# Head roots by logarithm, hyena chunks in quarters, and a convolution and spectrum products straight from PSUM, in the second block of a two-block model

## The reference

```
q = apply_rope_2(split_heads_norm(q, q_norm, 8 heads), cos, sin)     # RMS norm over 128 per head
k = apply_rope_2(split_heads_norm(k, k_norm, 2 heads), cos, sin)
p = softmax(q @ concat(k_ctx, k).T * 128**-0.5);  attn = p @ concat(v_ctx, v)

def short_conv(u, w, bias):                     # three taps, per channel, over tokens
    up = pad(u, one token on each side)
    return up[:, :-2] * w[0] + up[:, 1:-1] * w[1] + up[:, 2:] * w[2] + bias
def hyena_mix(u, ...):
    x0, x1, v = split(short_conv(u, conv_w, conv_b), 3)   # 3 x 512 channels
    v = v * x1
    y = irfft(rfft(v, 512) * rfft(filter, 512))[:256] + v * bias    # complex product
    return y * x0
merged = sigmoid(g_a) * (attn @ w_o_attn) + sigmoid(g_h) * (hyena @ w_o_hyena)
```

## Time and profile before

| what | value |
|---|---|
| median of 3 runs | 2690.96 us (2687.08 to 2691.71) |
| profiled execution, its own time | 2687.02 us |
| its span | 2685.1 us |
| PE busy | 2540.7 us (95%) |
| DVE, ACT, POOL busy | 1263.0, 1266.3, 1472.4 us |
| chain that ended last | PE 81%, DVE 9%, ACT 4%, POOL 3% |

### The profile page before, as it was taken

The page is one execution under the profiler, slowest core; times in us unless marked ns, Lnnn a source line. Parts: engine busy times, 40 slices in busy tenths (PEclk is TensorE's granted clock), DMA queues, the critical chain, the costliest instruction groups (busy, mean ns, idle before and its releaser), DMA issues.

```text
span 2685.1 us, 42027 instructions
## 1 busy us (share of the span) xinstructions
PE 2540.7 (95%) x16564; PEld 2180.6 (81%) x16564; DVE 1263.0 (47%) x2162; ACT 1266.3 (47%) x2111; POOL 1472.4 (55%) x857
## 2 busy tenths in 40 slices
PE   6999999998999899999898999989999988989997
PEld 6997889988998789986576766766888867888997
DVE  7795744452975755444466422132101037635223
ACT  5467854355447963453533311342333344535543
POOL 6875746458975855454431123743555544463970
PEclk9999999999999999998999999999999999999999
DMA  5443343354544343353320112231222223135554
GB/s 222 179 173 142 114 155 140 142 188 170 183 167 157 110 173 142 112 191 126 141 79 32 48 64 78 94 114 66 94 94 94 95 108 110 70 120 189 174 188 142
DMA packets 50552, 347.63 MB, mean 129 GB/s; under 512 B 5312, under 2 KB 8640, under 8 KB 8896
## 3 DMA queue, kind: packets, MB, share of 16 engines
q1 hardware_dynamic: 47840, 340.31, 35.2%
q10 hardware_dynamic: 2528, 4.72, 0.5%
HBM read 343.96 MB, written 1.05 MB: 128 GB/s over the span
## 4 chain that ended last, share of the span: by engine, by line
PE 81%; DVE 9%; ACT 4%; POOL 3%; issue 2%; DMA 1%; SPq 0%; POOLq 0%; ACTq 0%; DVEq 0%
PE pg L1838 21%; PE pg L1839 20%; PE pg L1840 20%; PE pg L1863 2%; PE ps L2127 2%; POOL ring_lo L643 2%; PE ps L2148 2%; PE ps L2146 1%; PE pg L1861 1%; PE ps L2286 1%; ACT ring_hi L755 1%; PE ps L1959 1%; PE ps L2358 1%; DVE big L1669 1%; PE ps L2267 1%
## 5 line engine op out<-in xcount | busy, mean ns | idle before, releaser
L643 POOL TENSOR_TENSOR ring_lo<-ring,ring_hi 128x1024 fp32r<-128x1024 f32 (+3 forms) x500 | 1167.3, 2348 | 803.7 <-ACT ring_hi L755 803.5
L1838 PE MATMUL pg<-HH,ring_hi 128*128 128x256 f32 (+1 forms) x3360 | 1077.9, 321 | 54.4 <-DVE HL L1309 16.3
L1839 PE MATMUL pg<-HH,ring_lo 128*128 128x256 f32 (+1 forms) x3360 | 1031.8, 307 | 0.0
L1840 PE MATMUL pg<-HL,ring_hi 128*128 128x256 f32 (+1 forms) x3104 | 958.7, 309 | 0.0
L1838 PEld LDWEIGHTS pg<-HH,ring_hi 128*128 128x128 f32 x3360 | 643.1, 191 | 138.5 <-issue 68.5
L1839 PEld LDWEIGHTS pg<-HH,ring_lo 128*128 128x128 f32 x3360 | 644.4, 192 | 42.9 <-issue 14.8
L1840 PEld LDWEIGHTS pg<-HL,ring_hi 128*128 128x128 f32 x3104 | 595.2, 192 | 30.8
L755 ACT ACTIVATE ring_hi<-ring 128x1024 fp32r<-128x1024 f32 (+6 forms) x564 | 555.0, 1002 | 33.6 <-DMA ring<-in_w_stream_dram 32.8
L765 ACT ACTIVATE take<-pg 128x256 f32<-128x256 f32 (+1 forms) x268 | 113.7, 425 | 497.7 <-PE pg L1840 446.3
L1840 PE MATMUL pg<-big_r,ring_hi 128*128 128x256 f32 (+1 forms) x864 | 275.3, 319 | 0.0
L1838 PE MATMUL pg<-big_r,ring_hi 128*128 128x256 f32 (+1 forms) x736 | 241.1, 328 | 7.3 <-DVE big_r L1778 3.1
(11 more groups left out here) (324 smaller groups left out, 3371.6 us busy)
## 6 DMA issues: line engine op xcount, KB each, us to landing
ring<-in_w_stream_dram SPq DMA_DIRECT2D x320, 1024.0 KB, 4.8
hn<-in_consts_dram ACTq DMA_DIRECT2D x2, 1024.0 KB, 5.9
cst<-in_consts_dram SPq DMA_DIRECT2D x1, 1472.0 KB, 19.6
prm<-in_params_dram SPq DMA_DIRECT2D x1, 1110.0 KB, 7.4
X<-in_xT_dram SPq DMA_DIRECT2D x1, 1024.0 KB, 5.8
X<-in_ctxT_dram ACTq DMA_DIRECT2D x1, 1024.0 KB, 5.7
out_dram<-H ACTq DMA_DIRECT2D x1, 1024.0 KB, 4.8
cst<-in_consts_dram SPq DMA_DIRECT2D x1, 768.0 KB, 16.5
```

What stands on the lines that cost most here:

```text
L643: pool.tensor_tensor(ring_lo[:, slot, cols], ring[:, slot, cols], ring_hi[:, place * P:(place + n) * P].bitcast(F32), SUB).then_inc(sem(LO ...
L1838: first = pe.matmul(out, a[0], b[0], start=start, stop=False)
L1839: pe.matmul(out, a[1], b[0], start=False, stop=False)
L1840: return first, pe.matmul(out, a[0], b[1], start=False, stop=stop)
```

## The change

**Head roots.** The square root and the reciprocal of the three head norms of a block-two layer become a logarithm and an exponential with scale -0.5, both on ACT (the way block one already had). `log_exp_tables` asks for the table set ahead of each root.

**Order.** The rope of K moves behind q2 chunk 4, those of heads 0 to 3 behind v2 chunk 0, the last two behind hy2 chunks 1 and 2. PE waits for earlier ropes before it writes the sums of the next norm, since both use `ps`. The third norm's sum moves from v2 chunk 1 to v2 chunk 2.

**Quarters.** The hy2 chunks beside attention are given out in quarters of two tiles; five of the 32 quarters go to the first two steps, the rest is spread.

**Convolution.** ACT writes the middle tap with its bias straight to the destination (Identity with scale and bias); DVE adds the two outer taps with `pg` as an operand. `hraw` and its padding go. A bank of `pg` is now free when DVE's convolution is done (`hconv`), not when ACT has drained it.

**Spectrum.** `VFT` is `ps` itself; ACT's copy goes.

```diff
 def att2_fill(l):
-    return spread([("hy2", l, j) for j in range(EARLY_HY, 12)], STEPS2[l] + LAG + 1)
+    parts = []
+    for j in range(EARLY_HY, 12):
+        x = ("hy2", l, j)
+        parts += [("part", x)] * (n_parts("hy2") - 1) + [x]
+    points = STEPS2[l] + LAG + 1
+    return [parts[0:3], parts[3:5]] + spread(parts[5:], points - 2)
...
-        VFT = hn[:, :].rearrange("p (a b) -> p a b", a=4)
+        VFT = ps[:, :, :]
...
-        ROPES_AFTER = [[0], [1], [2], [3, 4]]
+        ROPES_AFTER = [[], [3], [4], []]
...
             def hyena_in(l, j):
                 n, ns = N_TOK[l], N_SEQ[l]
-                ahead(CHUNK["hy2", l, j])
-                if 12 * l + j >= 2:
-                    act.wait_ge(sem("hconv"), 12 * l + j - 1)
-                s0 = (j % 2) * 2
-                act.activation(hraw[:, s0:s0 + ns, 1:T + 1],
-                               ready(CHUNK["hy2", l, j])[:, 0:n].rearrange("p (s t) -> p s t", s=ns), ACT.Copy)\
-                    .then_inc(sem("drained"), 1)
+                w = (l * 12 + j) * HY_TAPS
+                act.activation((X0, X1, VX)[j // 4][:, j % 4, 0:n], ready(CHUNK["hy2", l, j])[:, 0:n], ACT.Identity,
+                               bias=PR("conv_b", l * 12 + j), scale=PR("conv_w", w + 1)).then_inc(sem("hy_first"), 1)
...
-                elif by_log(i):
+                else:
                     inverse_root(hn[:, 0:cols], ps_flat[:, 0:cols], eps6, scale, "hn_rms")
-                else:
-                    act.activation(hn[:, 0:cols], ps_flat[:, 0:cols], ACT.Sqrt, bias=eps6, scale=scale).then_inc(sem("hn_rms"), 1)
...
-                    act.wait_ge(sem("vf_ready"), 2 * l + s + 1)
-                    act.activation(VFT, ps[:, :, :], ACT.Copy).then_inc(sem("vf_done"), 1)
...
-                    if not by_log(i):
-                        link(dve.reciprocal(r, r))
...
-                link(dve.tensor_scalar(dst, hraw[:, s0:s0 + ns, 0:T], PR("conv_w", w), PR("conv_b", l * 12 + j), MUL, ADD))
+                link(dve.scalar_tensor_tensor(dst[:, :, 1:T], src[:, :, 0:T - 1], PR("conv_w", w), dst[:, :, 1:T], MUL, ADD))
                 yield
-                link(dve.scalar_tensor_tensor(dst, hraw[:, s0:s0 + ns, 1:T + 1], PR("conv_w", w + 1), dst, MUL, ADD))
-                yield
-                ins = dve.scalar_tensor_tensor(dst, hraw[:, s0:s0 + ns, 2:T + 2], PR("conv_w", w + 2), dst, MUL, ADD)
+                ins = dve.scalar_tensor_tensor(dst[:, :, 0:T - 1], src[:, :, 1:T], PR("conv_w", w + 2), dst[:, :, 0:T - 1], MUL, ADD)
...
-                    dve.wait_ge(sem("vf_done"), k + 1)
+                    dve.wait_ge(sem("vf_ready"), k + 1)
...
+                    elif name == "hy2":
+                        pe.wait_ge(sem("hconv"), 12 * l + i + 1)
...
+                def rot2(jj):
+                    pe.wait_ge(sem("hn_done"), i + (1 if jj == 0 else 2 if jj < 3 else 3))
+                    rot(ROPE2[l] + jj, C("rot2"), Q2_[:, 2 * jj - 2:2 * jj, 0:T] if jj else K2_[:, :, 0:T])
                 for j in range(8):
                     chunk("q2", l, j, KD, hx, n)
                     if j == 1:
                         head_norm(i, 1024)
+                    if j == 4:
+                        rot2(0)
                     if j == 5:
                         pe.wait_ge(sem("hn_rms"), i + 1)
+                        pe.wait_ge(sem("rope"), ROPE2[l] + 1)
                         head_norm(i + 1, 4 * n)
...
-                    if tt == 1:
+                    if tt == 0:
                         pe.wait_ge(sem("hn_rms"), i + 2)
+                        rot2(1)
+                        rot2(2)
+                    if tt == 2:
+                        pe.wait_ge(sem("rope"), ROPE2[l] + 3)
                         head_norm(i + 2, 4 * n)
```

More of the change, by code:

```diff
@@ L282, in chunk_order @@
         add("hy2", 0, EARLY_HY)
-        out += sum(att2_fill(l), []) + sum(hyena_fill(l), [])
+        out += whole(sum(att2_fill(l), [])) + sum(hyena_fill(l), [])
         add("oh", 0, 16)
@@ L302 @@
 for x in ORDER:
-    count += x[0] != "dn"
+    count += x[0] not in ("dn", "hy2")
     DRAINED[x] = count
@@ L573, in build @@
         MGQ = H[:, :, T:2 * T]
-        ROPES_AFTER = [[0], [1], [2], [3, 4]]
+        ROPES_AFTER = [[], [3], [4], []]
         FILTER_1 = [0, 2, 4, 6, 7]
         FILTER_2 = [0, 1, 2, 3, 4]
-        def by_log(i):
-            return i < HN_BASE2[0]
         def in_place(i):
-            return by_log(i) and i % 6 != ATT_N
+            return i < HN_BASE2[0] and i % 6 != ATT_N
         def x_done(i, m=KD - 1):
@@ L715, in _ @@
                 for h in range(HEADS if l == DEPTH - 1 else 0):
-                    done = sum(att2_fill(l)[:(HIGH_AT + [ATT_STEPS + LAG])[h] + 1], [])
+                    done = whole(sum(att2_fill(l)[:(HIGH_AT + [ATT_STEPS + LAG])[h] + 1], []))
                     if done:
@@ L1159, in _ @@
                         attention2_exp(IT2_BASE[l] + k, steps[k][1])
-                    drain_fill(items)
+                    drain_fill(whole(items))
                     if LAG <= k < len(steps) + LAG:
@@ L1707, in hyena_conv @@
                 n, ns = N_TOK[l], N_SEQ[l]
[L1708 to L1710 removed]
+                dve.wait_ge(sem("hy_first"), 12 * l + j + 1)
+                dst, src = (b.rearrange("p (s t) -> p s t", s=ns) for b in ((X0, X1, VX)[j // 4][:, j % 4, 0:n],
+                                                                          pg[:, CHUNK["hy2", l, j] % 4, 0:n]))
                 w = (l * 12 + j) * HY_TAPS
[L1712 removed]
+                link(dve.scalar_tensor_tensor(dst[:, :, 1:T], src[:, :, 0:T - 1], PR("conv_w", w), dst[:, :, 1:T], MUL, ADD))
                 yield
[L1714 to L1716 removed]
+                ins = dve.scalar_tensor_tensor(dst[:, :, 0:T - 1], src[:, :, 1:T], PR("conv_w", w + 2), dst[:, :, 0:T - 1], MUL, ADD)
                 if j >= 8:
@@ L1733, in _ @@
                 all_of(head_norm(i, K2_, PR("k_norm", l)))
+                rope2(l, 0)
                 all_of(head_norm(i + 1, Q2_[:, 0:4, 0:n], PR("q_norm", l)))
+                rope2(l, 1)
+                rope2(l, 2)
                 all_of(head_norm(i + 2, Q2_[:, 4:8, 0:n], PR("q_norm", l)))
@@ L1749, in _ @@
                         attention2_out(i - LAG - 1, steps[k - LAG - 1])
-                    for name, l_, j in items:
+                    for name, l_, j in whole(items):
                         convs.append(hyena_conv(l, j))
```

19 lines of the change are left out of this document (4 added, 15 removed).

## The result

The changed kernel took 2647.11 us (median of 4 runs, 2645.97 to 2649.29) against 2690.4 us (4 runs, 2687.08 to 2691.71) on the same chip: ratio 0.9842, 95% interval 0.9827 to 0.9858. Its profiled execution has a span of 2644.4 us, 40.7 less than that of before. The forecast of 2650 us held, and so did the lengths named for the two attention stretches, but one step behind them did not: the convolution was priced at nothing of its own, and it carried much of the gain.

What follows compares the result with a forecast made beforehand. Block two was taken as bound by latency between engines, leaving PE waiting or at slower clock. 6.9 + 25.2 + 6.6 = 38.7 us off 2687.02 gives 2648.3, forecast as 2650 us given run spread; own range 2643 to 2656.

Steps and rivals of the forecast that it cites:

- Most that could return: PE time lost in block two's attentions, ahead of attention and in layer 1's spectrum: 45.7 us at most.
- Leftover in attention: PE waits that remain in both attentions despite quarters: 5 us, bounds 0 and 14.
- Convolution: Two DVE operations with one PSUM operand replace three: never slower, gain counted inside the attention sum without its own size.
- Quarters: In both attentions, quarter chunks cover PE's usual pauses: 30.2 - 5 = 25.2 us come back.
- Roots and ropes: Ahead of attention, shorter logarithm norms and moved ropes remove waits and slow clock: 8.9 - 2 = 6.9 us come back.
- new waits for finished ropes: Ahead of attention, PE waits for ropes before the next norm's sums: 2 us, bounds 0 and 7.5.
- Spectrum: Layer 1, forward to inverse transform: without ACT's copy and product outliers, all 6.6 us come back.
- The chain's pace: Rival in attention: the round through DVE and ACT still sets the pace; half of 30.2 us stay, 2658 to 2662; chance 0.16.
- the ropes at their bound: Rival ahead of attention: rope waits 7.5 us instead of 2, plus two slow-clock stretches, 2659 us; chance 0.08.
- banks freed by DVE: Rival: chunk starts wait for DVE's convolution four chunks back, 60 us lost, 2708 us; chance of slower 0.03.
- slow PSUM products: Rival in layer 1's spectrum: four PSUM products cost twice, the wait becomes 7 us, 2658 us; chance 0.04.
- a chunk's quarter of over 1.5 us: Sign in the profile after that the prediction was wrong; a quarter was priced at 1.42 or 0.71 us.

Runs made afterwards that it cites:

- sbuf_convolution: Changed kernel with the old convolution: ACT copies the chunk to SBUF, DVE does three operations there; 2668.3 us, ratio 0.992.
- only_quarters: Kernel before with only the hy2 chunks in quarters, five of them in the first two steps; 2677.2 us, ratio 0.995.
- no_gpsimd_split: Changed kernel with the old SBUF convolution, GpSimd writing zeros instead of splitting block two's hyena and gate weights; 2646.2 us, ratio 0.984.

## Why the prediction was right, point by point

- **Most that could return.** 45.7 us were counted, by packing PE's starts. 41.8 came. The packed length of attention of layer 0, 98.0 us, is PE's busy time there now (97.98), and no stretch came out shorter than its packed length. This method held best of all.
- **Leftover in attention.** 5 us was taken, 3.4 measured: 99.61 - 98.0 = 1.6 and 59.16 - 57.4 = 1.8.
- **Convolution: the step that failed.** "Forms with two SBUF inputs have outliers of two to three times. So it is never slower ... I count the gain inside the attention sum." The direction was right and the price absent. Taken out of the changed kernel it costs 21 us (18.5 by the stretches), alone it gives 14 (2689.7 to 2675.3). The outliers had been seen, though the rope's longest is 4.3 times its shortest there and not two to three, and not asked for their cause; "never POOL" was true of PE's waits and hid that POOL was holding DVE.
- **Quarters.** 25.2 us were credited to them, 26.9 came in the two attentions, but not from them alone: quarters alone give 10.4 (9.2 + 1.1), the convolution alone 2.7 (4.1 - 1.3), both together with the rest 26.9. So some 14 us are there only when both are in; the logarithm alone gives the attentions nothing (0.7 us more), but the rest without both was not run. The runs above give the reason: in quarters the first SBUF operation of nearly each convolution meets a split, and with the convolution in PSUM it passes. That the total came out all the same is in part luck: the price that the convolution lacked was credited to the quarters, and both were in the change.
- **Roots and ropes.** 6.9 us were credited, 8.1 came (7.0 + 1.1). In layer 1 the logarithm alone returns 1.5, the convolution alone 7.8 with the old roots and order. The logarithm with the new order and an SBUF convolution (sbuf_convolution) returns 7.0 ahead of attention and loses 3.6 of them in attention, against only_quarters. So the mechanism of the prediction works in part and was not needed: the ropes were late behind a convolution of 7.4 us. Moving them ahead of it removes their wait but leaves DVE late; shortening it removes both. The new waits for finished ropes, taken at 2 us, are 0.4.
- **Spectrum.** 6.6 us forecast, 6.8 measured, and 7.2 by undoing it. Of its four PSUM products none has an outlier.
- **Rivals.** The chain's pace, the ropes at their bound, banks freed by DVE and slow PSUM products did not occur: no PE wait names a convolution. The rope's long forms did appear, up to 2.76 us, without a wait. A rival was missing: that the quarters bring POOL's and DVE's operations together. The change was safe from it only through its other edit.

Named as a sign that it would be wrong was a chunk's quarter of over 1.5 us. That sign says little: a step with a quarter costs what its tiles cost, 1.42 us in layer 0 by the starts, and the sums of the stretches decide.

The front part says that engines meet only at semaphores. These runs show one exception: DVE and GpSimd hold each other up with no semaphore between them. The Trainium skill's page "SBUF — State Buffer", section "Who interferes with whom", covers this: a VectorE instruction with two SBUF inputs contends with a GpSimd instruction that reads SBUF but not with one that only writes, one in a 2-port mode contends with any, and whichever started first holds the other off for its whole length. This case's traces agree: DVE ends 0.27 to 1.08 us after POOL in the rows above, somewhat less than it needs alone (0.54 to 1.22). Beside the memsets of no_gpsimd_split the operations with two SBUF inputs passed (0.75 us) and the tensor_scalar waited (0.77 in place of 0.54), as the page has it if the tensor_scalar runs in a 2-port mode. No view names the mode; the durations fit it, since 256 more columns cost the tensor_scalar 0.13 us (0.41 to 0.54) and the form with two inputs 0.26 (0.48 to 0.74).

The page "VectorE: DVE Perf Modes", section "Rules for kernel authors", offers, as one of two ways, a copy from PSUM to SBUF ahead of many operations. Here, for float32 beside a busy GpSimd, both measurements go against it: 8 us for the spectrum, 21 us for the convolution.

## What to carry to other kernels

When one line's durations have a long tail, find what runs beside the long ones before pricing any edit that touches it; a wait table shows who released an engine, not who held the releaser. On this kernel DVE's operands decide: with one of its two inputs in PSUM it passes GpSimd's splits, with all in SBUF it stands until the split is done. Finer interleaving can make two engines meet at every step that used to miss each other, so each edit is to be measured both alone and taken out: here some 14 us belonged to neither edit by itself, and the gain ahead of attention could be had by either of two.

## What the runs showed of the hardware that was not expected

- A GpSimd operation of 128x1024 on two SBUF tensors (2.36 us) holds a DVE operation that takes 0.54 us alone until 2.2 us are over (0.74 and 2.47 us in the other form), and a GpSimd memset of 0.96 us holds the first form to 0.77 us but not the other one (0.75 us).
- ACT's drain from PSUM with scale and bias by pointer takes 0.56 us for 256 and 0.77 us for 512 columns, where the plain copy took 0.39 and 0.60; the prediction had 0.47 for 256 from its nearest row.
- Removing 52 us of DVE work (the reciprocals) did not move the time: 0.9992.
